# Expert rows stored block by block and gathered at the end, and x turned by VectorE instead of TensorE

## The reference, cut to what matters

```
s = sigmoid(x @ w_router); 8 of 64 experts per token (group-limited top-k), weights wts
xb  = x_pad[row_tok]              # rows sorted by expert, blocks of 128 rows, one expert per block
hid = silu(xb @ w_gate[e]) * (xb @ w_up[e])          # 1024 -> 256
yb  = hid @ w_down[e]                                # 256 -> 1024
y   = segment_sum(yb * row_w, row_tok)               # eight rows per token are added up
out = layer_norm(alpha * x + y + shared(x)) 
```

## Time and profile before

| | us |
|---|---|
| median of 3 runs (3031.73 to 3036.44) | 3032.62 |
| the profiled execution, its own time | 3045.78 |
| its span, first to last instruction | 3044.1 |
| `shared_and_route`, 1700.88 to 1875.63 | 174.75 |
| `block_tables`, 1875.63 to 1884.73 | 9.10 |
| `experts`, 1884.73 to 2996.55 | 1111.82 |
| `final_norm`, 2996.55 to 3044.10 | 47.55 |

### The profile page before, as it was taken

The page is one execution under the profiler, slowest core; times in us unless marked ns, Lnnn a source line. Parts: engine busy times, 40 slices in busy tenths (PEclk is TensorE's granted clock), DMA queues, the critical chain, the costliest instruction groups (busy, mean ns, idle before and its releaser), DMA issues. The chain is left out here.

```text
span 3044.1 us, 44781 instructions
## 1 busy us (share of the span) xinstructions
PE 2569.8 (84%) x14616; PEld 2151.4 (71%) x14617; DVE 1835.4 (60%) x2585; ACT 1330.3 (44%) x1859; POOL 775.0 (25%) x901
## 2 busy tenths in 40 slices
PE   3989998998999899969969741899999988998891
PEld 3867777777777777847858631787777877887781
DVE  2246787778688755536536531566656677555745
ACT  2243454355345333325322100566656667555741
POOL 2002221221321111100002063334333433333333
PEclk7989999999999999989989875999999999999996
DMA  4533345532323244253543235999999999899974
GB/s 89 72 48 60 56 51 61 63 56 43 70 53 60 58 76 78 67 192 109 166 169 118 73 39 134 284 271 291 268 282 258 298 296 332 242 273 263 331 180 149
DMA packets 346841, 462.88 MB, mean 152 GB/s; under 512 B 22568, under 2 KB 278056, under 8 KB 346734
## 3 DMA queue, kind: packets, MB, share of 16 engines
q1 hardware_dynamic: 311966, 343.37, 43.1%
q0 software_dynamic: 34768, 118.05, 14.9%
HBM read 367.21 MB, written 94.10 MB: 152 GB/s over the span
## 5 line engine op out<-in xcount | busy, mean ns | idle before, releaser
L57 PE MATMUL gu_ps<-e_hi,xg_hi 128*128 128x256 f32 x1488 | 437.5, 294 | 30.0 <-DVE e_lo L2254 16.4
L57 PE MATMUL dn_pj<-x_hi,dn_hi 128*128 128x512 f32 x1024 | 438.4, 428 | 21.7 <-DVE dn_lo L888 21.7
L59 PE MATMUL gu_ps<-e_hi,xg_lo 128*128 128x256 f32 x1488 | 423.8, 285 | 0.0
L58 PE MATMUL gu_ps<-e_lo,xg_hi 128*128 128x256 f32 x1488 | 423.4, 285 | 0.0
L59 PE MATMUL dn_pj<-x_hi,dn_lo 128*128 128x512 f32 x1024 | 410.9, 401 | 0.0
L58 PE MATMUL dn_pj<-x_lo,dn_hi 128*128 128x512 f32 x1024 | 409.7, 400 | 0.0
L972 DVE SCALAR_TENSOR_TENSOR uc_half<-u_in,par,uc_half 128x512 f32<-128x512 f32 x480 | 383.6, 799 | 13.1
L2195 ACT ACTIVATE e_hi<-e_raw 128x1024 fp32r<-128x1024 f32 x256 | 266.3, 1057 | 168.2 <-DMA e_raw<-in_w_up_e_dram 167.7
L57 PEld LDWEIGHTS gu_ps<-e_hi,xg_hi 128*128 128x128 f32 x1488 | 289.0, 194 | 58.4 <-DVE e_lo L2254 31.3
L2254 DVE TENSOR_TENSOR e_lo<-e_raw,e_hi 128x1024 fp32r<-128x1024 f32 x256 | 303.4, 1220 | 40.1 <-ACT e_hi L2195 39.4
L58 PEld LDWEIGHTS gu_ps<-e_lo,xg_hi 128*128 128x128 f32 x1488 | 287.3, 193 | 1.2
(11 more groups left out here) (346 smaller groups left out, 5232.6 us busy)
## 6 DMA issues: line engine op xcount, KB each, us to landing
e_raw<-in_w_gate_e_dram SPq DMA_DIRECT2D x256, 256.0 KB
e_raw<-in_w_up_e_dram SPq DMA_DIRECT2D x256, 256.0 KB
e_raw<-in_w_down_e_dram SPq DMA_DIRECT2D x128, 512.0 KB
dn_raw<-in_w_in_dram SPq DMA_DIRECT2D x64, 512.0 KB
gate_rows<-qkv_next SPq DMA_DIRECT2D x16, 512.0 KB, 3.0
br_raw<-in_w_oa_dram SPq DMA_DIRECT2D x16, 512.0 KB
br_gate<-gate_rows SPq DMA_DIRECT2D x32, 256.0 KB, 4.2
br_raw<-in_w_ob_dram SPq DMA_DIRECT2D x16, 512.0 KB
```

The costliest lines, as they stand in the source:

```text
L57: nc.tensor.matmul(out, w_hi, x_hi, start=first, stop=False)
L58: nc.tensor.matmul(out, w_hi, x_lo, start=False, stop=False)
L59: return nc.tensor.matmul(out, w_lo, x_hi, start=False, stop=last)
```

## The change

Experts: the result of a block is stored plainly, in block order, into a table `y_rows` of 139 blocks. The adding scatter is gone, and with it the four small copies of row numbers but one. The store runs three blocks behind the gather in GpSimd's order (`LAG`). The token's weight moves from the result to `hidden` (VectorE, one scalar_tensor_tensor of 256 columns). The x rows are gathered as four indirect DMAs of 1 KB quarters, laid out so that one VectorE transpose of 32x32 blocks (`x_turn`) turns them; the eight PE transposes go. Gate and up become one product of 512 columns (24 matmuls), and down of a block is issued behind gate and up of the next one. Gate and up weights are loaded in separate 4 KB runs. In ScalarE's and VectorE's order, four of the six pieces of the weights two experts ahead stand ahead of the block's own work, two behind it.

Final norm: for each tile of 128 tokens GpSimd gathers eight rows per token (64 indirect DMAs of 0.5 MB in all, four sets of buffers); VectorE adds three of the eight, TensorE sums five through the identity, and VectorE adds that sum; the bias moves to VectorE.

Around it: `delta_net` copies rows of x into the unused end of `y_rows` (nine DRAM-to-DRAM copies of 4 MB or less, SyncE), the row numbers for the end are made in `shared_and_route`, and `block_tables` makes four row tables where it made one.

```diff
@@ delta_net, SyncE
+                def fill_rows(q):
+                    b0 = LAG + E + q * NT
+                    n = min(NT, YB - b0) * P
+                    if n > 0:
+                        sp.dma_start(self.yr_d[b0 * P:b0 * P + n, :], a["x"][0, 0:n, :]).then_inc(rows_filled, 16)
...
                     u_half(g, p)
+                    fill_rows(q)
@@ shared_and_route, VectorE
+                step(v.tensor_scalar(nbc[:], nbc[:], float(P), float(LAG * P + 1), ALU.mult, ALU.add))
+                step(tt(vr[:], pos_ps[:], nbc[:].unsqueeze(1).to_broadcast([P, NT, E]), ALU.add))
+                step(tt(vr[:], vr[:], se[:], ALU.mult))
+                for t in range(NT):
+                    last = v.max(r8[:, t, :], vr[:, t, :])
+                step(last)
+                step(v.tensor_scalar(self.y_row[:], fl(r8[:]), 1.0, None, ALU.subtract))
                 hidden(1)
@@ experts, GpSimd
+                def gather(n):
+                    pool.wait_ge(idx_c, n + 1)
+                    for rb in range(4):
+                        alone(pool, self.passed)
+                        pool.indirect_dma_start(xq[:, rb].rearrange("p i k -> p (i k)"), None, x_quarters,
+                                                bass.IndirectOffsetOnAxis(idx[:, rb:rb + 1], 0)).then_inc(xg_in, 16)
+                def store(n):
+                    pool.wait_ge(y_ready, n + 1)
+                    alone(pool, self.passed)
+                    pool.dma_start(self.yr_d[bass.ds(n * P, P), :], yb[:]).then_inc(stored, 16)
...
+                        pool.wait_ge(t_done, n + 1)
+                        alone(pool, self.passed)
+                        g.tensor_copy(idx[:], self.idx_tab[...]).then_inc(idx_c, 1)
+                        gather(n)
+                        store(n)
@@ experts, TensorE
+                def blk(e, j, j_prev, gb, first):
+                    pe.wait_ge(xl_s, gb * 2 + 1)
+                    if first:
+                        pe.wait_ge(lo_s, e * PIECES + 2)
+                    gate_up(j, range(0, 4))
+                    pe.wait_ge(xl_s, gb * 2 + 2)
+                    if first:
+                        pe.wait_ge(lo_s, e * PIECES + 4)
+                    gate_up(j, range(4, 8)).then_inc(gu_done, 1)
+                    if j_prev is not None:
+                        down(j_prev, gb - 1)
+                    hid_t(gb)
@@ experts, ScalarE
+                def blk(gb, prev, split):
+                    split(0, 1, 2, 3)
+                    act.wait_ge(gu_done, gb + 1)
+                    A(sg[:], gu[:, 0, :], ACT.Silu).then_inc(sg_s, 1)
+                    act.wait_ge(t_done, gb + 3)
+                    x_hi(0)
+                    x_hi(1)
+                    if prev:
+                        y_move(gb - 1)
+                    act.wait_ge(ht_done, gb + 1)
+                    A(hh[:], ht[:], ACT.Copy).then_inc(hh_s, 1)
                     split(4, 5)
@@ experts, VectorE
+                def x_turn(gb):
+                    if not isinstance(gb, int) or gb:
+                        dve.wait_ge(xl_s, gb * 2)
+                    dve.wait_ge(xg_in, gb * 64 + 64)
+                    v.transpose(xt[:].rearrange("p k (r j) -> p r k j", r=4), xq[:].rearrange("p r i k -> p r k i")
+                                ).then_inc(t_done, 1)
+                def blk(e, b, gb, split):
+                    split(0, 1, 2, 3)
+                    x_turn(gb + 1)
+                    dve.wait_ge(sg_s, gb + 1)
+                    v.scalar_tensor_tensor(out=hid[:], in0=sg[:], scalar=self.wt_tab[:, bass.ds(e * NT + b, 1)],
+                                           in1=gu[:, 1, :], op0=ALU.mult, op1=ALU.mult).then_inc(hid_s, 1)
                     x_lo(gb + 1, 0)
                     x_lo(gb + 1, 1)
+                    dve.wait_ge(hh_s, gb + 1)
+                    tt(hl[:], ht[:], hh[:].bitcast(F32), ALU.subtract).then_inc(hl_s, 1)
+                    split(4, 5)
@@ final_norm
+            def _(pool):
+                for i in range(NT):
+                    if i >= SETS:
+                        pool.wait_ge(added, ADDS * (i - SETS + 1))
+                    for r in range(TOPK):
+                        arrived = (dve_rows if r < TOPK - ON_PE else pe_rows)[i % SETS]
+                        pool.indirect_dma_start(rows[i % SETS][r][:], None, self.yr_d, ...).then_inc(arrived, 16)
+            def _(pe):
+                    for hf in range(2):
+                        for r in range(TOPK - ON_PE, TOPK):
+                            last = nc.tensor.matmul(ps[i % SETS][:, hf, :], self.ident[:], rows[i % SETS][r][...], ...)
+            def _(dve):
+                        for r in range(TOPK - ON_PE):
+                            add(i, r, rows[i % SETS][r][:])
+                        dve.wait_ge(pe_sum, i + 1)
+                        add(i, ADDS - 1, ps[i % SETS][:].rearrange("p a b -> p (a b)"))
```

348 lines of the change are left out of this document (148 added, 200 removed).

## The result

The change makes the kernel slower: 3419.7 us (median of 4 runs, 3409.9 to 3432.0) against 3034.5 on the same chip, a ratio of 1.127, 95% interval 1.124 to 1.129. The forecast was 3068. The profiled execution took 3422.7 us, its span is 3421.1.

A forecast was written before the change was run, and what follows sets the result against it. Experts were taken as bound by a serial round of scatter, landing, copy. Experts -57, final norm +82, block tables +6, routing +3, fills +1 gave +35 us on the 3032.6 median: 3068 us; range 2965 to 3150, the forecast's own 3040 to 3100.

The forecast's parts named there:

- Slower: Whole kernel: forecast sign, slower than before by more than the 6 us that count as no change; chance 0.59.
- The gather's round (9.6 us): Experts: copying row numbers, four gathers, last landing and x_turn make a serial round, ruling second blocks at 9.6 us.
- The busy row, 6.7 us: Experts: a gather in busy queues, 2289.47 to 2296.21, taken as upper bound of the landing, making the round 13.3 us.
- VectorE's order (12.8 us): Experts: VectorE's in-order work and waits, laid out, make two single-block experts in a row go at 12.8 us.
- The experts go at the pace of a serial round of scatter, landing, copy.: Experts before the change: a 12.0 us round of scatter, landing and copy sets the pace, against 11.95 us per block.
- C: Rival: the scatter was not the bound; experts keep 1112 us, +92, 3125 us in all; chance 0.08.
- the -57: Experts: forecast change of the stage, 1055 us against 1112.
- The final norm, block tables, routing: Stages outside the experts: final norm +82 us (129 against 47.6), block tables +6, routing +3.
- The fills (+1): Delta stage: nine 4 MB copies on SyncE's queue fit a 14.4 us gap at 10.7 us each; +1 us.
- rival D: Rival: the fills delay the delta stage, +60 us, 3128 us in all; chance 0.05.
- A: Rival, experts: VectorE's waits in order vanish, 902 us, 126 less; 2942 us in all, half of that 3005; chance 0.30.
- B: Rival, experts: quarters wait for weight packets, +130, 3198 us; or x_turn at 1.93 alone, +65, 3133 us; chance 0.14.

The follow-up runs named there:

- d2: Changed kernel, but from the second expert on only a quarter of the two down pieces is loaded: 3302.5 us, experts 1206.4.
- e6: Changed kernel with the VectorE transpose replaced by a plain copy of the same elements, x not turned: 3315.5 us, 1.089.
- d1: Changed kernel, but from the second expert on only a quarter of every weight piece is loaded: 3238.1 us, experts 1143.4.
- b1: Kernel before with gate and up weights in separate 4 KB runs and two result buffers, adding scatter kept: 3021.2 us, 0.995.
- b2: Same as b1, with the scatter's row numbers also copied ahead of the wait for the landing: 3044.1 us, 0.999.
- e4: Changed kernel with x gathered in one piece of 4 KB rows and turned by TensorE: 3138.0 us, 1.030, experts 1037.1.
- e3: Kernel before with only the nine fill copies added: 3106.8 us, 1.020, experts 1097.3 with their code unchanged.
- h1: Kernel before with only gate and up weights loaded in separate 4 KB runs: 3028.6 us, 0.998.
- b4: Same as b3, but with one result buffer: 2994.6 us, 0.987.
- b3: Kernel before with the change's order in the experts, adding scatter kept from two result buffers, x turned by TensorE: 2981.8 us, 0.983.

## Why the prediction was wrong
*The sign and the side.* Slower was right (0.59), the size was not: 341 us beyond the forecast for the profiled execution (3422.7 against 3081), of which 274 are the experts, 69 the fills, and the rest cancels.

*The gather's round (9.6 us): the step that failed.* Its landing was put at 2.8 us, from a gather alone in the queues, with the reason that "right after x_turn VectorE frees no weight slot for some 4 us, so the weight queue is nearly idle then". To the letter that was so: the turn ends at 2503.98, the first down piece goes out at 2508.58. But the fourth quarter is issued at 2509.69, between two down pieces of 0.5 MB. The window to look at reaches from the first issue to the last landing, 10.4 us, not 4. The busy row, 6.7 us, was on the page and was set aside; 6.0 to 6.2 is what came. With the down pieces cut down the landing is the 2.8 us of the forecast (d2). The fourth issue starts 4.4 us behind the first, not 3.8, because one issue of the four takes 1.5. And `x_turn` was put at 1.2 us, from an operation of the same size; it takes 2.05, nearer to the 2.5 that the prediction had worked out from the Trainium skill ("VectorE: DVE Perf Modes", The three transpose paths) and not used. The sum for a second block, 1.4 + 4.4 + 6.0 + 2.0 = 13.8, stands against 13.6 measured. Against the forecast the second blocks cost 29 x (13.57 - 9.6) = 115 us more, first blocks behind second ones 28 x (14.01 - 10.4) = 101, first behind first 36 x (14.13 - 12.8) = 48; with 7 at both ends and 2 for 36 and 28 in place of 35 and 29 that is the 274 (the terms are rounded). The turn is 79 of it (e6); the rest is the landing and the slower issues, less what VectorE's order hides of them.

*VectorE's order (12.8 us)* was right in size: 12.8 to 13.0 wherever the gather is out of the way (d1, d2), though with a turn 0.85 us longer, so that the rest of the order is that much shorter than laid out by hand. In the kernel as changed it lies 1.1 us under the gather's round, 14.1 where a first block follows a first one. The turn was to wait for the gather only on second blocks; it waits 92 times of 94.

*"The experts go at the pace of a serial round of scatter, landing, copy."* The reading was that a serial round of 12.0 us which equals the 11.95 us per block sets the pace, and C (the scatter was not the bound) had 0.08. The round was real, but equal lengths did not exclude a second one. TensorE's 89% busy was a hint, and so were the two waits of GpSimd that stood above those of the earlier trace rows in the same view. The earlier trace rows itself puts the copy at 2304.06 down to TensorE (`<-PE y_ps L59`) and not to the landing. Shortening the scatter's round alone brings nothing (b1, b2). The size of the -57 came out in e4 (-75, -60 against e3) partly by luck: some 36 of it come with the new order and its products while the scatter stays (h1 to b4), and 10 to 17 with the plain store. The step had also said that merging the halves saves nothing; TensorE's busy time is 60 us less with all parts of the order together, and its gate and up products alone are busy 32 us less (580.0 in b1, 547.6 in b3).

*The final norm, block tables, routing* were right to a microsecond or two: +82, +6, +3. Inside the norm two small errors cancel: the last rows are in 106 us into the stage, not 109.5, and what follows takes 23 us, not 20. One term is right by luck: the sum over ten matmuls was put at 9 us, as twice the 0.233 us for full float32 and twice again for the low level of the clock. No run shows that first factor; a tile's sum takes 8.85 us at a granted clock of 1.00 (from 3385.93), which is 0.885 us for a matmul of 512 columns.

*The fills (+1).* The step looked at what stands behind them on SyncE's queue, the next weight load. The load did come late, and did no harm that the waits show (13.4 us, 20.1 before). What was hit was a 256 KB store on GpSimd's queue that VectorE waits for. It was rival D in effect (+60), priced from another mechanism and given 0.05.

*Rivals.* A (VectorE's queue closes up) did not happen. B (turn and quarters cost more, 0.14) named the right place, but both of its halves make 195 of the 274 us. Its first half is 145 when redone, not 130: 29 rounds of 9.6 and 29 of 10.4 become 12.5. C (the scatter was not the bound) is what b1 and b2 show of the kernel before, though the experts without it did not keep their 1112 us (e4).

## What to carry to other kernels
Before a serial wait is bought out, ask what the stage would take without it: give it a second buffer, which costs little, and see whether the pace moves. Look at the longest waits of the same view too, not only at those that fit the round. A transfer's landing is priced from a busy row of the same queues unless the writer has listed every transfer that is issued in its window on any queue, and large copies that nobody waits for are cut into 4 KB packets, or they hold up the small ones that somebody does wait for.

## What the runs showed that I had not expected
- DRAM to DRAM copies in packets of 64 KB beside a 256 KB store make VectorE wait for that store up to 11.4 us (79.3 us over the stage); beside the same bytes in 4 KB packets it waits up to 4.2 (15.8).
- A transpose of 32x32 blocks over 128x1024 float32 takes VectorE 2.05 us, a copy of the same elements 0.69.
- An indirect DMA of 128 rows costs GpSimd 0.95 us and 0.30 to the next, at 4 KB, 2 KB and 1 KB rows alike, but one of four takes 1.5 in the experts, and an adding scatter 1.6 to 2.5 (b1 to b4); what stretches them was not tried.
- When the experts' TensorE idles in each round, its granted clock over the stage is 0.85 in place of 0.97; how much of the experts' time that is was not separated, since VectorE and the gather set the pace.
